# W_out's post-norm sums in two groups, with square 6 added on VectorE

## What is computed

```
def rmsnorm(x, g):
    y = xf * lax.rsqrt(jnp.mean(xf * xf, axis=-1, keepdims=True) + RMS_EPS)
    return (y * g.astype(jnp.float32)).astype(x.dtype)

def swiglu(x, w_in, w_out):
    gate, up = jnp.split(x @ w_in, 2, axis=-1)
    return (jax.nn.silu(gate) * up) @ w_out

for l in range(DEPTH):
    h = h + 0.5 * rmsnorm(swiglu(rmsnorm(h, g[FFN1_PRE]), ffn_w_in[l, 0], ffn_w_out[l, 0]), g[FFN1_POST])
    ...                      # token mixers, projected by W_o, with a post-norm too
    h = h + 0.5 * rmsnorm(swiglu(rmsnorm(h, g[FFN2_PRE]), ffn_w_in[l, 1], ffn_w_out[l, 1]), g[FFN2_POST])
```

## Time and profile before

| | |
|---|---|
| median of 3 runs | 1208.91 us (1208.87 to 1208.96) |
| the profiled execution | 1208.9 us, span from first to last instruction 1207.1 us |
| TensorE busy | 1192.8 us, 99% of the span |
| VectorE, ScalarE, GpSimd busy | 59%, 45%, 37% |
| granted TensorE clock, mean | 0.998 of full speed |
| DMA | 197.59 MB, mean 164 GB/s |

### The profile page before, as it was taken

How to read it: one execution, slowest core, us unless ns; L and a number is a source line. 1 busy time by engine, 2 the same in 40 slices (tenths; PEclk the granted TensorE clock), 3 DMA queues, 4 the chain that set the end, 5 groups by cost and what they waited for, 6 DMA issues and landing times.

```text
span 1207.1 us, 23892 instructions
## 1 busy us (share of the span) xinstructions
PE 1192.8 (99%) x9352; PEld 1156.5 (96%) x9352; DVE 717.1 (59%) x1034; ACT 540.3 (45%) x758; POOL 443.0 (37%) x520
## 2 busy tenths in 40 slices
PE   9999999999999999999999999999999999999997
PEld 7999999999999999999999999999999999999986
DVE  6655444758665765554477554447676667755542
ACT  6433334536653553333354333345366546434441
POOL 0754500306312375542128454113064124765500
PEclk9999999999999999999999999999999999999999
DMA  9654357462355465534636544564733553755540
GB/s 315 222 174 152 126 177 228 128 206 83 97 138 187 132 207 167 175 117 150 217 119 218 174 160 131 169 202 122 231 106 102 163 192 105 243 175 168 175 161 35
DMA packets 197614, 197.59 MB, mean 164 GB/s; under 512 B 4136, under 2 KB 190736, under 8 KB 197536
## 3 DMA queue, kind: packets, MB, share of 16 engines
q1 hardware_dynamic: 197088, 196.10, 51.5%
q10 hardware_dynamic: 448, 0.39, 0.1%
HBM read 195.43 MB, written 1.05 MB: 163 GB/s over the span
## 4 chain that ended last, share of the span: by engine, by line
PE 95%; DVE 2%; ACT 1%; issue 1%; DMA 0%; POOL 0%; ACTq 0%; DVEq 0%; POOLq 0%
PE bank L448 28%; PE bank L450 28%; PE bank L449 28%; PE bank L649 2%; PE bank L650 2%; PE bank L648 2%; PE bank L737 1%; PE bank L536 1%; PE bank L732 1%; PE bank L691 1%; PE bank L702 0%; DVE h L1254 0%; DVE tmp L1245 0%; DMA gates<-in_pool_scale 0%; PE bank L694 0%
## 5 line engine op out<-in xcount | busy, mean ns | idle before, releaser
L1156 DVE TENSOR_TENSOR w_lo<-raw,w_hi 128x2048 fp32r<-128x2048 f32 (+3 forms) x205 | 432.6, 2115 | 278.1 <-ACT w_hi L862 278.1
L448 PE MATMUL bank<-x_hi,w_hi 128*128 128x272 f32 (+1 forms) x2028 | 587.9, 290 | 0.6 <-DVE y L1360 0.2
L450 PE MATMUL bank<-x_hi,w_lo 128*128 128x272 f32 (+1 forms) x2028 | 581.5, 287 | 0.0
L449 PE MATMUL bank<-x_lo,w_hi 128*128 128x272 f32 (+1 forms) x2028 | 579.7, 286 | 0.0
L862 ACT ACTIVATE w_hi<-raw 128x2048 fp32r<-128x2048 f32 (+2 forms) x210 | 352.0, 1685 | 444.7 <-PE bank L450 433.9
L448 PEld LDWEIGHTS bank<-x_hi,w_hi 128*128 128x128 f32 x2028 | 382.1, 188 | 4.1 <-DVE x_lo L1236 2.6
L449 PEld LDWEIGHTS bank<-x_lo,w_hi 128*128 128x128 f32 x2028 | 382.0, 188 | 0.3
L450 PEld LDWEIGHTS bank<-x_hi,w_lo 128*128 128x128 f32 x2028 | 382.0, 188 | 0.0
L448 PE MATMUL bank<-hid_hi,w_hi 128*128 128x272 f32 x528 | 152.6, 289 | 0.0
L449 PE MATMUL bank<-hid_lo,w_hi 128*128 128x272 f32 x528 | 151.9, 288 | 0.0
L450 PE MATMUL bank<-hid_hi,w_lo 128*128 128x272 f32 x528 | 151.6, 287 | 0.0
(11 more groups left out here) (199 smaller groups left out, 1232.3 us busy)
## 6 DMA issues: line engine op xcount, KB each, us to landing
raw<-in_ffn_w_in SPq DMA_DIRECT2D x87, 1024.0 KB, 5.1
raw<-in_w_in SPq DMA_DIRECT2D x24, 1024.0 KB, 5.6
raw<-in_ffn_w_out SPq DMA_DIRECT2D x24, 768.0 KB, 4.4
raw<-in_ffn_w_out SPq DMA_DIRECT2D x24, 640.0 KB, 4.0
raw<-in_ffn_w_out SPq DMA_DIRECT2D x10, 1024.0 KB, 5.1
raw<-in_w_in SPq DMA_DIRECT2D x16, 512.0 KB, 5.2
raw<-in_w_attn_proj SPq DMA_DIRECT2D x32, 256.0 KB, 4.5
raw<-in_w_o SPq DMA_DIRECT2D x8, 1024.0 KB, 5.4
```

The lines of the kernel that those rows point to most:

```text
L448: pe.matmul(ps[:, t0:T], w[0], a_hi[:, t0:T], start=start, stop=False)
L449: pe.matmul(ps[:, t0:T], w[0], a_lo[:, t0:T], start=False, stop=False)
L450: return pe.matmul(ps[:, t0:T], w[1], a_hi[:, t0:T], start=False, stop=stop)
L1156: last = dve.tensor_tensor(lo, w, hi.bitcast(F32), ALU.subtract)
```

## The change

For q = 1 and 5 the sums go in two groups. VectorE adds square 6 to `acc` between the two parts of the low half that it makes there anyway (`split_lo_between` in place of `split_lo`; unit 2, so far one instruction, is cut in two). TensorE's group of `acc` moves from the start of tile 7 to the place ahead of its last three products, where the group of square 6 was, and that group is gone. `ADDS` counts VectorE's addition now; GpSimd makes the same five additions as before (`range(1, 6)`).

```
-SUM_PARTS = (1, 3, 1, 2, 1, 3)
-ADDS = (KD - 1, KD - 3, KD - 1, KD - 2, KD - 1, KD - 3)
+SUM_PARTS = (1, 2, 1, 2, 1, 2)
+ADDS = (KD - 1, KD - 2, KD - 1, KD - 2, KD - 1, KD - 2)
...
-                        if u == N_OUT - 1 and mt == 1:
-                            sum_part(4 * f + 1, l, 0)
                         for k in range(OUT_K[j]):
                             kk = OUT_K0[j] + k
                             if u == N_OUT - 1 and mt == 1 and kk == KF - 1:
-                                sum_part(4 * f + 1, l, 1)
+                                sum_part(4 * f + 1, l, 0)
...
-                sum_part(4 * f + 1, l, 2)
+                sum_part(4 * f + 1, l, 1)
...
                 def split_and_root(u, u_layer, q):
-                    split_lo(u, u_layer)
+                    split_lo_between(u, u_layer, lambda: add_square_6(q, l))
                     post_rms(q, l)
...
             def add_squares(q, l):
-                for m in range(1, ADDS[q] + (0 if q == 3 else 1)):
+                for m in range(1, ADDS[q] + 1 - q % 2):
```

## The result

The changed kernel takes 1210.95 us (median of 22 executions, 1209.87 to 1212.37) against 1208.93 for the kernel before (22 executions, 19 of them between 1208.73 and 1209.16). The ratio is 1.0015, 95% interval 1.0009 to 1.0021. So it is slower by about 2 us, inside the 0.2% that was called no difference, but clear of the noise of this comparison. The range's end, 1210.8, is 0.16% above the 1208.9 of the forecast: the ratio lies just inside it, the median itself 0.15 us outside. The forecast's own +0.4 covers a fifth of the change. And something is new: the kernel before repeats within 0.5 us in 19 of its 22 executions (the other three took 1211.7), the changed one scatters over 2.5.

The account below looks back on a forecast made before the run. TensorE, busy 99% of the span, was taken as the bound. Removing 0.67 us and adding a 0.81 us wait gave +0.13 per site, +0.4 on 1208.9: 1209.3 us, range 1208.1 to 1210.8, no measurable difference.

Parts of the forecast that it names:

- The forecast's own +0.4: Total over three sites, +0.13 us each: TensorE's new wait outweighs the removed group of sums.
- The removed group: TensorE's three sums of square 6, taken out once per site: 0.67 us each, 2.0 us in all.
- The wait: TensorE's acc group, ahead of tile 7's last three products, waits for VectorE's add: 0.81 us per site.
- rival 2: VectorE separates copy, half and add: 0.16 us per site, at most 1.3, so 1209.8 to 1213.2 us; chance 3%.
- The release: From the end of VectorE's add to TensorE's acc weight load: 0.05 us, range zero to 0.2.
- Rival 1: TensorE's clock falls to the 1.2 GHz level through the new wait: about 1217 us, 1213 to 1227; chance 4%.
- The price: Cost of a clock fall, from the wait through root and boundary: 2 to 3 us per site, up to 6.
- sites A, B and C: W_out's last unit in layer 0's first FFN (209 us), its second (611 us), layer 1's first (818 us).
- A time slower by over 0.2%: Whole kernel measurably slower: 6%, of it 4% from the clock and 2% from VectorE separating its steps.
- Rivals 3 and 4: TensorE doesn't wait, 1206.9 us, chance 3%; another wait (GpSimd's addition) holds both forms, 1208.9 us, chance 1%.
- the half's delay: VectorE's second half ends 0.35 us later; its idle time ahead of the root, 1.98 us, becomes about 1.75.
- The granted clock stays 1.00: Last-named sign that the forecast holds: TensorE's granted clock doesn't fall.

Follow-up runs that it names:

- the kernel with both waits filled: Changed kernel plus six products of real data ahead of the moved acc group and four ahead of the last square's group: 1209.57 us.
- the form with the addition first: Changed kernel with VectorE's addition of square 6 ahead of the whole low half, not between its parts: 1209.81 us median, in two groups.
- wait filled on the identity: Changed kernel plus three idle matmuls of 128 columns on the identity ahead of the moved acc group: 1210.61 us.
- addition last: Changed kernel with VectorE's addition of square 6 behind the whole low half: 1216.73 us, ratio 1.0066.
- dense rows behind: Changed kernel, wait unfilled, both rows of five idle matmuls around the root's spread replaced by ten products of real data each: 1212.36 us.
- addition first, dense rows behind: Changed kernel with the addition ahead of the whole low half and ten real-data products in each row around the root's spread: 1210.08 us.

## Why the prediction was right and where it was wrong

**The removed group: right.** 0.67 us per site was read from rows; the run without it gave 2.0 us in all.

**The wait: right in its place and nearly in size.** The add starts 211.35 - 209.86 = 1.49 after the copy, as taken from W_o (1.49). Counted as the prediction counted, from the start of the twelfth product to the load, the wait is 211.90 - 211.04 = 0.86 us against 0.81; the 0.79 in the row of the loads starts at the end of the load before. VectorE shows no gap between half and add (210.21 + 1.22 = 211.43, the add starts at 211.35), so rival 2 is out. This trace doesn't agree with a flush behind every instruction, as the prediction gave the rule of the Trainium skill ("VectorE: DVE Perf Modes", section "The DRAIN you can't avoid"). The same section says too that a next instruction that isn't held starts earlier, which the prediction left out; by these rows the add and the halves are such instructions.

**The release: mis-sized.** The add ends at 211.35 + 0.43 = 211.78 and the group loads at 211.90: 0.12 us, where 0.05 was taken from ScalarE's square. With it the sum would have been +0.20 per site; measured +0.18. The range for it (zero to 0.2) held. The part that doesn't depend on the clock is +0.55 and not +0.4: 1209.5 us, which the kernel with both waits filled shows (1209.57).

**The clock: the step that failed.** Rival 1 had 4% and happened: in the profiled execution at one of three sites, and by the times, all of which lie above 1209.5, in nearly every execution. Its reason in the prediction was that the clock stood at 1.00 in the same stretch with 0.58 us idle. That was a row about less idleness than the change makes; that it was near an edge, no row of before could show, and the argument took the absence of falls for a margin. A wait of 0.32 us is enough: the form with the addition first shows it by its times, and by two falls in the trace that has dense rows behind the sums.

The price was put at 2 to 3 us per site, up to 6. The ten falls at these sites in the traces cost this much. The cost is counted from tile 7's last product to the next stage's first (5.02, 4.96 and 5.02 us at sites A, B and C before), beginnings and lengths are read from windows of 0.1 us:

| kernel | site | begins behind that last product, us | lasts, us | costs, us |
|---|---|---|---|---|
| changed | C | 1.3 | 3.5 | 1.21 |
| wait filled on the identity | B | 1.9 | 3.5 | 0.64 |
| the same | C | 2.2 | 3.5 | 0.37 |
| addition last | A | 0.4 | 6.9 | 1.84 |
| the same | B | 2.0 | 3.6 | 0.58 |
| the same | C | 1.3 | 3.5 | 1.27 |
| dense rows behind | A | 0.7 | 6.9 | 2.17 |
| the same | C | 0.9 | 6.9 | 1.97 |
| addition first, dense rows behind | A | 1.6 | 3.5 | 1.07 |
| the same | B | 2.2 | 3.5 | 0.85 |

So the price isn't one number: about 2 us is right for a long fall, and a short one with the idle rows behind the sums costs less the later it begins. Site C of the changed kernel shows why. The loss sits in the first row of idle matmuls (823.14 to 825.41, 2.27 us, against 1.36) and in the spread (0.64 to the next row against 0.37), together 1.18. Behind the spread TensorE waits for the boundary's first tile anyway: the second row of idle matmuls only eats into that wait (0.45 in place of 0.66), and by the dense products the clock is back. A fall that begins later lies more in that second part.

That the measured ratio still lies just inside the range is luck: two errors offset each other in it, too small a chance and, for the falls that happened, mostly too high a price. A time slower by over 0.2% was meant for exactly this mechanism; it needs 1.9 us of lost work over the three sites, and most executions lose less.

**The rest.** Rivals 3 and 4 are out: TensorE waits, for VectorE's acc. VectorE's idle time ahead of the root is 1.83 (1.75 foretold), so the half's delay is covered. From tile 6's copy to tile 7's first square it is 213.25 - 209.86 = 3.39 us (3.33 foretold). "The granted clock stays 1.00", the sign that was named last, is the one that didn't come.

**Open.** Why the clock falls in one execution at one site and in another at none can't be read: a profile shows one execution. That real products in both waits keep it is shown by the times (1209.57, eight of eleven within 0.23 us, against 1210.95). That they do it better than matmuls on the identity rests on less: in the first wait alone, medians of 1210.06 and 1210.61 that overlap, and one trace each. Matmuls on the identity in both waits are an untested rival, and whether it is the identity's zeros, the narrower moving operand or the fp32 format was not parted.

## What to carry to other kernels

Count a wait that is put on TensorE twice: once as time against what it replaces, and once for what it can do to the clock together with the light stretches next to it (here sums with one moving column and a wait for a square). The kernel may have been near a fall of the clock that no trace of it shows, and a wider scatter of the executions is the sign. When work is moved onto an engine that releases TensorE, put it ahead of that engine's long step and not in the middle: here the short add behind the square alone made the wait 0.32 us in place of 0.79; then fill what wait is left with dense products that fit inside it.

## What the runs showed of the hardware

- Three matmuls on the identity (128 moving columns, fp32) in the new wait left no gap there in TensorE's records, and the granted clock fell to 0.50 at two of three sites all the same; six products of hid_hi with 272 columns in the same place held it in the profiled execution, and the median was 0.55 us lower. With four more in the next wait eight of eleven executions agreed within 0.23 us.
- A fall of the clock lasted 3.5 or 6.9 us in these traces and cost 0.4 to 2.2 us, by when it began. It could begin in the middle of a row of products with 272 columns (616.9, in a row that began at 616.02).
- At the lower clock five matmuls on the identity took 2.48 us in place of 1.36, ten products of 272 columns 2.61 in place of 1.51.
- From the recorded end of VectorE's add on acc (128x272) to TensorE's weight load 0.12 us passed; from VectorE's last step of the root (128x3) 0.05, the same as from ScalarE's square. So the trace of the kernel before held a row for VectorE's way to a weight load, and it would have been too short for the add:

```profile
215.11 0.16 DVE L1218 SCALAR_TENSOR_TENSOR rt<-halved,near 128x3 f32<-128x3 f32 x1
...
215.32 0.30 PEld L557 LDWEIGHTS bank<-ident,rt 128*128 128x128 f32 x3 [0.19 <-DVE rt L1218]
```
